# First attention of a two-layer trunk: the two key tiles' scores merged to 128 columns before the exponentials

## The chip, the core and the metric

The kernel runs on one NeuronCore of one Trainium2 chip. The metric is the device time of one execution in microseconds. Before the change the median of three runs is 3507.34 us (3507.19 to 3508.57).

## The reference, cut to what matters

The program computes a two-layer decoder trunk. The first layer is sliding-window attention with learned sinks, on 2048 tokens and 16 meta tokens, 16 query heads of 64 and 2 key heads; after it come routed experts, a second attention, experts again and a final norm. Only the first attention is touched. For a block of 128 queries and one head it computes

```
keys  = [16 meta | 128 of the previous block | 128 of the own block]      # 272 scores
mask  : meta always; previous block where k > q (not for the first block); own block where k <= q
m     = max(max over scores, sink)
p     = exp(s - m) / (sum(exp(s - m)) + exp(sink - m))
o     = p @ values of the 272 keys
```

For one query row, key column c of the previous block is allowed exactly where c > q, and column c of the own block exactly where c <= q. So of each pair of columns (c of the previous, c of the own block) at most one is allowed.

## The kernel before, in words

`attention_a` walks over NT = 17 tiles of 128 rows (tile 0 holds the meta tokens). A tile has 8 pairs (k = 0..7) of two heads, one head of each key head (g = 0, 1), so there are NP = 136 pairs q = 8n + k. Four pairs are one group H of 8 heads. Each engine runs its own written-out list over q; they meet in semaphores only.

In step q the engines do this, in this order:

- TensorE: the scores of pair q into PSUM `S[q % 2]` (L635, three passes for the split of fp32 into high and low part; it waits for `masked` of q - 2). Then one job for a later tile: k = 0, 1 transposes of the input x of tile n + 2 (L576); k = 2, 4, 7 its projection by 512, 512 and 256 columns (L590 to L592, 24 matmuls each); k = 3, 5 transposes of the queries of tile n + 1 (L602), k = 6 of its keys (L608). Then the transposes of the probabilities of pair q - 6 (L649, four of 128x128; after the last pair of a group one more for the meta keys, L654), and the products with the values of pair q - 7 (L668; at a group's end those with the meta values, L677).
- VectorE: scale, mask and row minimum of the negated scores of pair q, one custom instruction for each of the two heads with its read of the accumulator (L538), which gives `z` and `negmax`. At a group's end the argument of the sink's exponential (L544); one step later denominators and reciprocals (L499, L501). Then the job: low parts of x (L452), of the queries (L470) and keys (L479, L480), the bias add after a projection (L461, L464). Then the copy of the transposed probabilities of pair q - 6 out of PSUM, for even pairs (L555), the meta one (L560), and before the scores at q % 4 = 3 the copy of the finished outputs O (L508).
- ScalarE: the job (high parts, L369, L384, L394, L395), the exponentials of pair q with row sums (L431), the sink's (L436), the copy of the transposed probabilities of odd pairs (L444), squares of x (L377, at k = 5).
- GpSimd: scaling of a group's probabilities by the reciprocals (L334 twice, L335), rotary embedding (L321, L322, L324, L351, L358), and the norm's factor (L310, L312).
- SyncE: loads and stores.

There is one PSUM tile PRJ for all the jobs. The second job of a kind waits for VectorE's last read of the first: projection k = 2 for both low parts of x, projection k = 4 for the low part of the queries made at k = 3, projection k = 7 for the low part of the keys made at k = 6, and the transposes of k = 3, 5 and 0 for the bias add before. `PT` is one PSUM tile of two banks, `pT` has three buffers.

Of the kernel before, what the change touches and what calls it, by code (L numbers as in the profile page):

```python
# [16 lines left out]
P = 128  # L17
# [132 lines left out]
def attention_a(nc, io, dram):  # L150


    with ExitStack() as ctx:
# [4 lines left out]
        GW = [512, 512, QKV - 1024]  # L158
        w_hi, w_lo = s.sb("w_hi", [P, DC, QKV], F32R), s.sb("w_lo", [P, DC, QKV], F32R)
# [21 lines left out]
        z = s.sb("z", [P, 2, 2, BAND])  # L181
        prob = s.sb("prob", [P, 3, 4, 2, BAND])
        pmeta = s.sb("pmeta", [P, 2, P])
        pT = s.sb("pT", [P, 3, 4 * P])
        pmT = s.sb("pmT", [P, 2, P])
        negmax = s.sb("negmax", [P, 2, 8])
# [6 lines left out]
        spare = prob[:, :, :, :, :].rearrange("p a i g k -> p (a i g k)")  # L193
        staged = [spare[:, QKV * k:QKV * k + QKV] for k in range(5)]
# [33 lines left out]
        copied_dve, copied_act = s.sem("copied_dve"), s.sem("copied_act")  # L228
# [3 lines left out]
        NCONST = 3  # L232
# [10 lines left out]
        with nc.Block() as block:  # L243
            @block.sync
            def _(sp):
# [30 lines left out]
                sp.dma_start(mask[:, :, :], io["mask_a"].rearrange("(t p) k -> p t k", p=P)).then_inc(consts, 16)  # L276
                load_tables(0)
# [18 lines left out]
            def _(pool):  # L296
# [30 lines left out]
                def scale(H):  # L327
                    pool.wait_ge(den_ready, H + 1)
                    if H >= 2:
                        pool.wait_ge(flipped, 5 * (H - 2) + 5)  # L330
                    heads, by = prob[:, H % 3, :, :, :].rearrange("p i g k -> p (i g) k"), rden[:, H % 2, :, :].rearrange("p i g -> p (i g)")
                    for c in range(2):
                        band = heads[:, 4 * c:4 * c + 4, META:BAND]
                        nc.gpsimd.tensor_tensor(band, band, by[:, 4 * c:4 * c + 4].unsqueeze(2).to_broadcast([P, 4, 2 * P]), ALU.mult).then_inc(scaled, 1)  # L334
# [29 lines left out]
            def _(act):  # L364
# [53 lines left out]
                for q in range(NP + 6):  # L418
                    n, k = divmod(q, PAIRS)
                    job(n, k)  # L420
# [17 lines left out]
                    if 0 <= u < NP:  # L438
                        H, i = divmod(u, 4)
                        if i % 2:  # L440
                            act.wait_ge(flipped, flips(u))
                            if u >= 3:
                                act.wait_ge(summed, pv_count(u - 3))
                            nc.scalar.copy(pT[:, u % 3, :], PT[:, 1, :]).then_inc(copied_act, 1)  # L444
# [4 lines left out]
            def _(dve):  # L449
# [53 lines left out]
                def keep_o(H):  # L503
                    n, b = divmod(H, 2)
                    dve.wait_ge(summed, 5 * H + 5)
                    if n >= 2:
                        dve.wait_ge(o_out[n % 2], 16 * (n // 2))
                    nc.vector.tensor_copy(oT[:, n % 2, 512 * b:512 * b + 512], O[:, :]).then_inc(o_ready, 1)  # L508

# [17 lines left out]
                for q in range(NP + 8):  # L527
                    n, k = divmod(q, PAIRS)
                    if q % 4 == 3 and q >= 11:
                        keep_o((q - 11) // 4)  # L530
                    if q < NP:
                        H, i = divmod(q, 4)
                        dve.wait_ge(scored, q + 1)
                        if q >= 2:
                            dve.wait_ge(exped, q - 1)
                        for g in range(2):
                            j = 2 * i + g
                            last = nc.vector.tensor_tensor_reduce(out=z[:, q % 2, g, :], in0=S[:, q % 2, g, 0:BAND], in1=mask[:, min(n, 2), :],  # L538
                                                                  scale=-A_SCALE, scalar=negsinks[:, 2 * k + g:2 * k + g + 1], op0=ALU.add, op1=ALU.min,
                                                                  accum_out=negmax[:, H % 2, j:j + 1])  # L540
                        last.then_inc(masked, 1)
                        if i == 3:
                            dve.drain()
                            nc.vector.tensor_tensor(sarg[:, H % 2, :], psinks[:, 8 * (H % 2):8 * (H % 2) + 8], negmax[:, H % 2, :], ALU.add).then_inc(sink_in, 1)  # L544
                    if q % 4 == 0 and 4 <= q <= NP:
                        denominators(q // 4 - 1)
                    job(n, k)
                    u = q - 6
                    if 0 <= u < NP:
                        H, i = divmod(u, 4)  # L550
                        if i % 2 == 0:
                            dve.wait_ge(flipped, flips(u))
                            if u >= 3:
                                dve.wait_ge(summed, pv_count(u - 3))
                            nc.vector.tensor_copy(pT[:, u % 3, :], PT[:, 0, :]).then_inc(copied_dve, 1)  # L555
                        if i == 3:
                            dve.wait_ge(flipped, 5 * H + 5)
                            if H >= 2:
                                dve.wait_ge(summed, 5 * (H - 2) + 5)
                            nc.vector.tensor_copy(pmT[:, H % 2, :], PT[:, 0, 0:P]).then_inc(copied_dve, 1)  # L560

            @block.tensor
            def _(pe):
# [60 lines left out]
                for q in range(NP + 7):  # L624
# [15 lines left out]
                    if 0 <= u < NP:  # L640
                        H, i = divmod(u, 4)
                        pe.wait_ge(scaled, 3 * H + 1 + i // 2)
                        if i % 2 == 0 and u >= 2:
                            pe.wait_ge(copied_dve, 3 * H + i // 2)
                        if i % 2 == 1 and u >= 2:
                            pe.wait_ge(copied_act, 2 * H + i // 2)
                        for a in range(4):
                            g, b = divmod(a, 2)
                            last = nc.tensor.transpose(PT[:, i % 2, P * a:P * a + P], prob[:, H % 3, i, g, META + P * b:META + P * b + P], ident[:, :])  # L649
                        last.then_inc(flipped, 1)  # L650
                        if i == 3:
                            pe.wait_ge(scaled, 3 * H + 3)
                            pe.wait_ge(copied_dve, 3 * H + 2)
                            nc.tensor.transpose(PT[:, 0, 0:P], pmeta[:, H % 2, :], ident[:, :]).then_inc(flipped, 1)  # L654
                    u = q - 7
                    if 0 <= u < NP:
                        H, i = divmod(u, 4)
                        m = u // PAIRS
                        if i % 2:
                            pe.wait_ge(copied_act, 2 * H + i // 2 + 1)  # L660
                        else:
                            pe.wait_ge(copied_dve, 3 * H + i // 2 + 1)
# [9 lines left out]
                        if i == 3:  # L672
                            if H == 0:
                                pe.wait_ge(vm_ready, 16 * 8)
                            pe.wait_ge(copied_dve, 3 * H + 3)
# [1859 lines left out]
def shape_constants():  # L2535
# [5 lines left out]
    def table(dim):  # L2541
# [25 lines left out]
        "mask_a": mask.reshape(3 * P, BAND),  # L2567
        "mask_b": np.where(k <= q, 0, MASKED).astype(bf),
# [26 lines left out]
```

## Time and profile before

| What | Value |
|---|---|
| median of three runs | 3507.34 us |
| profiled execution | 3507.11 us, its span 3505.3 us |
| mean granted TensorE clock | 0.946 |
| first attention | first scores at 74.8 us, last output copy ends at 604.9 us |
| busy, whole span | TensorE 90%, VectorE 50%, ScalarE 36%, GpSimd 51% |

The page of the profile gives busy shares over the whole span and in 40 slices of 87.6 us. The first attention is slices 1 to 7. For it the timeline of single engines (start, duration, instruction, and in brackets the idle time before it and what ended that) and the busy times of chosen stretches are read. An instruction's start minus the start of the one before it is what it takes of its engine; its own duration is longer, since instructions overlap.

### The profile page before, as it was taken

The numbers are of one execution on the slowest core, as the hardware profiler recorded it, in microseconds if no ns is written. First come the engines' busy times: TensorE is split into PE (matmuls) and PEld (weight loads), VectorE is DVE, ScalarE is ACT, GpSimd is POOL, SyncE is SP. The second block draws the span as 40 slices with busy tenths as digits, with TensorE's granted clock in tenths as the row PEclk, the third lists the DMA queues.
The fourth block names the chain that finished last, engine by engine and source line by source line (L and its number), as shares of the span: only waits on it lengthen the run. The fifth ranks groups of instructions, "written<-read, shape, count | busy, mean of one in ns | idle before, by whom it ended". The sixth has DMA issues, their size and how long they took to land. (4 is left out here: it accounts for less than half of the span.)

```text
span 3505.3 us, 57395 instructions
## 1 busy us (share of the span) xinstructions
PE 3156.1 (90%) x19855; PEld 2492.3 (71%) x19855; DVE 1742.2 (50%) x3672; ACT 1244.6 (36%) x2673; POOL 1791.3 (51%) x1445
## 2 busy tenths in 40 slices
PE   6999998898799995999799999999998978999950
PEld 4788886787688885898566666666656867888840
DVE  3555555677343333665445555555535653433316
ACT  2444444332222222444344444444343222222212
POOL 2555554344344441454598888888871223444312
PEclk8999999999899997999799999999999989999975
DMA  2001111643898884787410221022005429999818
GB/s 102 27 27 40 39 34 38 210 155 114 302 333 309 301 298 135 236 269 216 113 37 25 52 52 50 13 52 52 10 10 198 161 94 347 363 318 314 276 67 329
DMA packets 358879, 535.93 MB, mean 153 GB/s; under 512 B 82881, under 2 KB 278997, under 8 KB 351780
## 3 DMA queue, kind: packets, MB, share of 16 engines
q1 hardware_dynamic: 331716, 457.26, 40.5%
q0 software_dynamic: 26976, 76.27, 5.6%
q8 instruction: 105, 1.72, 0.2%
q14 instruction: 82, 0.67, 0.1%
HBM read 397.13 MB, written 144.92 MB: 155 GB/s over the span
## 5 line engine op out<-in xcount | busy, mean ns | idle before, releaser
L2105 POOL TENSOR_TENSOR ab_acc<-ab_acc,ab_pT 128x1024 f32<-128x1024 f32 (+2 forms) x320 | 593.6, 1855 | 93.2 <-ACT ab_pT L2139 55.9
L2139 ACT ACTIVATE ab_pT<-ab_S 128x512 f32<-128x512 f32 (+4 forms) x704 | 350.2, 504 | 518.0 <-PE ab_S L2223 252.8
L2155 DVE TENSOR_REDUCE ab_mx<-ab_W 128x2 f32<-128x1024 f32 (+5 forms) x352 | 348.7, 995 | 363.1 <-PE ab_W L2238 219.9
L1264 POOL DMA_INDIRECT scratch_y<-ex_y,ex_prow x64 | 64.8, 1013 | 492.0 <-issue 353.1
L1434 PE MATMUL ex_G<-ex_xT,ex_wg 128*128 128x160 f32 x2048 | 293.3, 302 | 2.6 <-DMA ex_wu<-in_moe_w_up 2.6
L1434 PE MATMUL ex_U<-ex_xT,ex_wu 128*128 128x160 f32 x2048 | 288.6, 299 | 0.0
L1434 PEld LDWEIGHTS ex_G<-ex_xT,ex_wg 128*128 128x128 f32 x2048 | 281.7, 191 | 7.6 <-issue 3.5
L2221 PE MATMUL ab_S<-ab_q_hi,ab_k_hi 97*128 97x512 f32 (+4 forms) x704 | 279.0, 396 | 5.3 <-ACT ab_pT L2139 3.6
L1434 PEld LDWEIGHTS ex_U<-ex_xT,ex_wu 128*128 128x128 f32 x2048 | 281.7, 190 | 0.0
L2275 PE MATMUL ab_O<-ab_pT,ab_v 128*64 128x512 f32 (+3 forms) x1280 | 261.3, 547 | 0.0
L2222 PE MATMUL ab_S<-ab_q_lo,ab_k_hi 96*128 96x512 f32 (+4 forms) x704 | 254.2, 361 | 0.0
L2223 PE MATMUL ab_S<-ab_q_hi,ab_k_lo 96*128 96x512 f32 (+4 forms) x704 | 252.6, 359 | 0.0
L1080 PE MATMUL pr_PR<-pr_wo_hi,pr_o_hi 128*128 128x512 f32 x528 | 217.1, 411 | 34.8 <-DVE pr_wo_lo L947 30.4
L334 POOL TENSOR_TENSOR aa_prob<-aa_prob,aa_rden 128x1024 f32<-128x1024 f32 x68 | 127.3, 1894 | 191.7 <-DVE aa_rden L501 191.7
L2238 PE MATMUL ab_W<-ab_k_hi,ab_q_hi 96*128 96x512 f32 (+5 forms) x704 | 207.1, 378 | 16.4 <-ACT ab_k_hi L2127 14.2
L1305 DVE TENSOR_TENSOR ex_wd_lo<-ex_wd,ex_wd_hi 128x2048 fp32r<-128x2048 f32 x64 | 146.7, 2292 | 137.6 <-ACT ex_wd_hi L1286 100.4
L1082 PE MATMUL pr_PR<-pr_wo_hi,pr_o_lo 128*128 128x512 f32 x528 | 210.0, 398 | 0.0
L1081 PE MATMUL pr_PR<-pr_wo_lo,pr_o_hi 128*128 128x512 f32 x528 | 208.3, 395 | 0.0
L1247 POOL DMA_INDIRECT ex_x<-scratch_xn,ex_grow x64 | 172.0, 2688 | 70.5 <-DVEq L1317 52.8
L2221 PEld LDWEIGHTS ab_S<-ab_q_hi,ab_k_hi 97*128 97x128 f32 x704 | 135.5, 193 | 84.4 <-issue 56.6
L2275 PEld LDWEIGHTS ab_O<-ab_pT,ab_v 128*64 128x64 f32 x1280 | 86.5, 139 | 139.6 <-issue 110.9
L1291 ACT ACTIVATE ex_act_g<-ex_G 128x320 f32<-128x320 f32 x64 | 28.0, 437 | 429.6 <-PE ex_U L1434 429.6
(315 smaller groups left out, 7082.3 us busy)
## 6 DMA issues: line engine op xcount, KB each, us to landing
ex_wg<-in_moe_w_gate SPq DMA_DIRECT2D x64, 1024.0 KB
ex_wu<-in_moe_w_up SPq DMA_DIRECT2D x64, 1024.0 KB
ex_wd<-in_moe_w_down SPq DMA_DIRECT2D x64, 1024.0 KB
pb_y<-scratch_y SPq DMA_DIRECT2D x17, 1024.0 KB
pr_o<-scratch_oT SPq DMA_DIRECT2D x33, 512.0 KB
scratch_h<-pr_h SPq DMA_DIRECT2D x33, 512.0 KB
scratch_xn<-pr_xn SPq DMA_DIRECT2D x33, 512.0 KB, 2.7
fi_y<-scratch_y SPq DMA_DIRECT2D x16, 1024.0 KB, 14.0
```

The source lines that it names most:

```text
L1080: nc.tensor.matmul(PR[:, b, :], o_hi[:, i.slot, c, :], wo_hi[:, c, w], start=(c == 0), stop=False)
L1081: nc.tensor.matmul(PR[:, b, :], o_hi[:, i.slot, c, :], wo_lo[:, c, w], start=False, stop=False)
L1082: return nc.tensor.matmul(PR[:, b, :], o_lo[:, i.slot, c, :], wo_hi[:, c, w], start=False, stop=(c == DC - 1))
L1434: last = nc.tensor.matmul(out[:, f.slot, CAP * k:CAP * k + CAP], w[:, f.slot4, c, P * k:P * k + P], xT[:, f.slot, c, :], start=(c == 0), s ...
L2105: nc.gpsimd.tensor_tensor(to, to, pT[:, U % RING, :, 0:n], ALU.add).then_inc(added, 1)
L2139: nc.scalar.activation(pT[:, U % RING, h, 0:n], S[:, h, 0:n], ACT.Exp, scale=B_SCALE).then_inc(exped, 1)
L2155: nc.vector.reduce_max(mx[:, :, t, c:c + 1].rearrange("p h a -> p (h a)"), W[:, j % 2, :, 0:n], AX.X).then_inc(emptied, 1)
L2221: nc.tensor.matmul(to, k_hi[:, p % 2, h, kb], q_hi[:, p % 2, h, qs], start=True, stop=False)
L2222: nc.tensor.matmul(to, k_hi[0:QD, p % 2, h, kb], q_lo[:, p % 2, h, qs], start=False, stop=False)
L2223: last = nc.tensor.matmul(to, k_lo[:, p % 2, h, kb], q_hi[0:QD, p % 2, h, qs], start=False, stop=not diagonal)
L2238: last = nc.tensor.matmul(W[:, j % 2, h, 0:n], q_hi[0:QD, p % 2, h, P * t:P * t + P], k_hi[0:QD, p % 2, h, lo:lo + n], start=True, stop=no ...
L2275: last = nc.tensor.matmul(O[HD * h:HD * h + HD, G % 2, 512 - n:512], values(U, h), pT[:, U % RING, h, 0:n], start=(U == opens[p, g]), stop ...
```

## The change

The 16 meta columns and the previous block (SPAN = 144 columns) are masked into `z`, the own block's 128 columns into a second tile `zc`, each by its own custom instruction with row minimum; the second takes the first's minimum as its starting value. An elementwise minimum then merges `zc` into `z`. Exponentials, scaling and transposes work on 144 and 128 columns in place of 272 and 256. The transposed probabilities are parted again when they are copied out of PSUM: two multiplications with the 0/1 masks `apart` (bf16), one for each block. That copy is VectorE's for every pair now; the copies of O and of the meta probabilities go to ScalarE.

```diff
+        SPAN = META + P
+        z = s.sb("z", [P, 2, 2, SPAN])
+        zc = s.sb("zc", [P, 2, 2, P])
+        apart = s.sb("apart", [P, 2, P], BF16)
+        stage = s.sb("stage", [P, 5 * QKV])
+        prob = stage[:, 0:3 * 8 * SPAN].rearrange("p (a i g k) -> p a i g k", a=3, i=4, g=2)
 # SyncE
+                sp.dma_start(apart[:, :, :].rearrange("p b q -> p (b q)"), io["apart_a"]).then_inc(consts, 16)
 # GpSimd, scale
-                        band = heads[:, 4 * c:4 * c + 4, META:BAND]
+                        band = heads[:, 4 * c:4 * c + 4, META:SPAN]
 # ScalarE
+                def keep_o(H):
+                    n, b = divmod(H, 2)
+                    act.wait_ge(summed, 5 * H + 5)
+                    if n >= 2:
+                        act.wait_ge(o_out[n % 2], 16 * (n // 2))
+                    nc.scalar.copy(oT[:, n % 2, 512 * b:512 * b + 512], O[:, :]).then_inc(o_ready, 1)
+                    if q % 4 == 3 and q >= 11:
+                        keep_o((q - 11) // 4)
...
-                            nc.scalar.copy(pT[:, u % 3, :], PT[:, 1, :]).then_inc(copied_act, 1)
+                    if 0 <= u < NP and u % 4 == 3:
+                        act.wait_ge(flipped, 5 * H + 5)
+                        nc.scalar.copy(pmT[:, H % 2, :], PT[:, 0, 0:P]).then_inc(copied_m, 1)
 # VectorE, pair q
-                            last = nc.vector.tensor_tensor_reduce(out=z[:, q % 2, g, :], in0=S[:, q % 2, g, 0:BAND], in1=mask[:, min(n, 2), :],
-                                                                  scale=-A_SCALE, scalar=negsinks[:, 2 * k + g:2 * k + g + 1], op0=ALU.add, op1=ALU.min,
-                                                                  accum_out=negmax[:, H % 2, j:j + 1])
-                        last.then_inc(masked, 1)
+                            nc.vector.tensor_tensor_reduce(out=z[:, q % 2, g, :], in0=S[:, q % 2, g, 0:SPAN], in1=mask[:, min(n, 2), 0:SPAN],
+                                                           scale=-A_SCALE, scalar=negsinks[:, 2 * k + g:2 * k + g + 1], op0=ALU.add, op1=ALU.min,
+                                                           accum_out=before[:, H % 2, j:j + 1])
+                        dve.drain()
+                        for g in range(2):
+                            nc.vector.tensor_tensor_reduce(out=zc[:, q % 2, g, :], in0=S[:, q % 2, g, SPAN:BAND], in1=mask[:, min(n, 2), SPAN:BAND],
+                                                           scale=-A_SCALE, scalar=before[:, H % 2, j:j + 1], op0=ALU.add, op1=ALU.min,
+                                                           accum_out=negmax[:, H % 2, j:j + 1])
+                        dve.drain()
+                        nc.vector.tensor_tensor(z[:, q % 2, :, META:SPAN], z[:, q % 2, :, META:SPAN], zc[:, q % 2, :, :], ALU.min).then_inc(masked, 1)
 # VectorE, pair u = q - 6
-                            nc.vector.tensor_copy(pT[:, u % 3, :], PT[:, 0, :]).then_inc(copied_dve, 1)
+                        for b in range(2):
+                            last = nc.vector.tensor_tensor(pT[:, u % 3, :].rearrange("p (g b q) -> p b g q", g=2, b=2)[:, b, :, :],
+                                                           PT[:, u % 2, 0:2 * P].rearrange("p (g q) -> p g q", g=2),
+                                                           apart[:, b, :].unsqueeze(1).to_broadcast([P, 2, P]), ALU.mult)
+                        last.then_inc(copied, 1)
 # TensorE, pair u = q - 6
-                        for a in range(4):
-                            g, b = divmod(a, 2)
-                            last = nc.tensor.transpose(PT[:, i % 2, P * a:P * a + P], prob[:, H % 3, i, g, META + P * b:META + P * b + P], ident[:, :])
+                        for g in range(2):
+                            last = nc.tensor.transpose(PT[:, i % 2, P * g:P * g + P], prob[:, H % 3, i, g, META:SPAN], ident[:, :])
```

The semaphores `copied_dve` and `copied_act` become `copied` (one count for each pair) and `copied_m` (one for each group). TensorE's products with the values are as before: four of 128x64 weights for each pair, and four with the meta values for each group.

## Rows read from the trace of the kernel before

**Rows 1.** Busy time by engine in one tile's stretch; then TensorE's clock:

```profile
303.98:336.17 32.19, 32.19 (x253) 26.02 (x251) 17.38 (x56) 14.57 (x48) 17.74 (x17) 1.00 0.11 36
```

**Rows 2.** Timeline of TensorE, the same tile: start, duration, line, operation:

```profile
303.98 0.50 PE L590 MATMUL aa_PRJ<-aa_w_hi,aa_x_hi 128*128 128x512 f32 x1
...
309.56 0.60 PE L649 MATMUL aa_PT<-aa_ident,aa_prob 128*128 128x128 f32 x4
...
311.77 0.40 PE L635 MATMUL aa_S<-aa_k_hi,aa_q_hi 64*128 64x272 f32 x2
...
314.52 0.50 PE L590 MATMUL aa_PRJ<-aa_w_hi,aa_x_hi 128*128 128x512 f32 x1
...
320.11 0.60 PE L649 MATMUL aa_PT<-aa_ident,aa_prob 128*128 128x128 f32 x4
...
321.23 0.39 PE L635 MATMUL aa_S<-aa_k_hi,aa_q_hi 64*128 64x272 f32 x2
...
327.03 0.39 PE L590 MATMUL aa_PRJ<-aa_w_hi,aa_x_hi 128*128 128x256 f32 x1
...
334.37 0.60 PE L649 MATMUL aa_PT<-aa_ident,aa_prob 128*128 128x128 f32 x4
334.81 0.27 PE L654 MATMUL aa_PT<-aa_ident,aa_pmeta 128*128 128x128 f32 x1
...
336.17 0.50 PE L590 MATMUL aa_PRJ<-aa_w_hi,aa_x_hi 128*128 128x512 f32 x1
```

**Rows 3.** Timeline of VectorE, the same tile:

```profile
309.76 0.75 DVE L461 SCALAR_TENSOR_TENSOR aa_qk<-aa_PRJ,aa_rstd,aa_bqkv 128x512 f32<-128x512 f32 x1 [4.74 <-PE aa_PRJ L592]
...
326.63 0.68 DVE L555 COPY aa_pT<-aa_PT 128x512 f32<-128x512 f32 x1
327.23 0.68 DVE L508 COPY aa_oT<-aa_O 128x512 f32<-128x512 f32 x1
...
328.25 0.50 DVE L538 CUSTOM_DVE_ANT_0 aa_z<-aa_S,aa_mask,aa_negsinks 128x272 f32<-128x272 f32 x1
328.67 0.08 DVE L538 DVE_READ_ACCUMULATOR2_ANT aa_negmax<- 128x1 f32 x1
328.84 0.17 DVE L544 TENSOR_TENSOR aa_sarg<-aa_psinks,aa_negmax 128x8 f32<-128x8 f32 x1
```

**Rows 4.** Groups by shape on VectorE, whole span: busy, mean ns, idle before:

```profile
L1305 DVE TENSOR_TENSOR ex_wd_lo<-ex_wd,ex_wd_hi 128x2048 fp32r<-128x2048 f32 x64 | 146.7, 2292 | 137.6 <-ACT ex_wd_hi L1286 100.4 <-issue 37.2
L1305 DVE TENSOR_TENSOR ex_h_lo<-ex_h,ex_h_hi 128x256 fp32r<-128x256 f32 x64 | 27.2, 425 | 5.0
L1022 DVE CUSTOM_DVE_ANT_0 pr_junk<-pr_hot,pr_place 128x32 f32<-128x32 f32 x66 | 12.7, 192 | 7.6
```

**Rows 5.** Timeline of a later stage, GpSimd and VectorE side by side:

```profile
779.57 2.39 POOL L870 TENSOR_TENSOR pr_res<-pr_res,pr_bo 128x1024 f32<-128x1024 f32 x1
...
779.62 3.43 DVE L1037 SCALAR_TENSOR_TENSOR pr_xn<-pr_h,pr_rstd,pr_gain 128x1024 f32<-128x1024 f32 x1 [1.29 <-POOL pr_rstd L880]
```

**Rows 6.** Timeline of GpSimd in the tile of rows 2:

```profile
321.14 1.27 POOL L321 TENSOR_TENSOR aa_rot<-aa_qk,aa_cs 128x512 f32<-128x512 f32 x1 [1.02 <-DVE aa_qk L461]
...
323.79 2.37 POOL L324 TENSOR_TENSOR aa_qk<-aa_qk,aa_cs 128x1024 f32<-128x1024 f32 x1
326.30 2.39 POOL L351 TENSOR_TENSOR aa_qr<-aa_qk,aa_rot 128x1024 f32<-128x1024 f32 x1
```

**Rows 7.** Timeline of TensorE at the stage's start:

```profile
79.70 0.50 PE L590 MATMUL aa_PRJ<-aa_w_hi,aa_x_hi 128*128 128x512 f32 x1 [0.82 <-DVE aa_x_lo L452]
...
88.40 0.52 PE L590 MATMUL aa_PRJ<-aa_w_hi,aa_x_hi 128*128 128x512 f32 x1 [0.83 <-DVE aa_q_lo L470]
...
92.13 0.41 PE L590 MATMUL aa_PRJ<-aa_w_hi,aa_x_hi 128*128 128x512 f32 x1
```

**Rows 8.** Busy time and clock in half a microsecond there, columns as rows 1:

```profile
89.00:89.50 0.50, 0.50 (x2) 0.39 (x2) 0.41 (x4) 0.28 (x1) 0.00 (x0) 0.50 0.00 0
```

**Rows 9.** L538 in the last two tiles: durations ns min/median/max, first and last start:

```profile
L538 DVE CUSTOM_DVE_ANT_0 aa_z<-aa_S,aa_mask,aa_negsinks x32: 491/498/501, 557.4 to 591.8; 128x272 f32<-128x272 f32 x32
```

More of the change, by code:

```diff
@@ L185, in attention_a @@
         pmT = s.sb("pmT", [P, 2, P])
+        before = s.sb("before", [P, 2, 8])
         negmax = s.sb("negmax", [P, 2, 8])
@@ L192, in attention_a @@
         oT = s.sb("oT", [P, 2, DC * P])
-        spare = prob[:, :, :, :, :].rearrange("p a i g k -> p (a i g k)")
-        staged = [spare[:, QKV * k:QKV * k + QKV] for k in range(5)]
+        staged = [stage[:, QKV * k:QKV * k + QKV] for k in range(5)]
         NS = len(staged)
@@ L231, in attention_a @@
         o_out = s.sems("o_out", 2)
-        NCONST = 3
+        NCONST = 4
         def live(n):
@@ L416, in _ @@
                         square(2)
-                for q in range(NP + 6):
+                def keep_o(H):
[4 more added lines that the diff above has]
+                    nc.scalar.copy(oT[:, n % 2, 512 * b:512 * b + 512], O[:, :]).then_inc(o_ready, 1)
+                for q in range(NP + 8):
                     n, k = divmod(q, PAIRS)
+                    if q % 4 == 3 and q >= 11:
+                        keep_o((q - 11) // 4)
                     job(n, k)
@@ L525, in _ @@
                     job(-1, k)
-                for q in range(NP + 8):
+                for q in range(NP + 6):
                     n, k = divmod(q, PAIRS)
-                    if q % 4 == 3 and q >= 11:
-                        keep_o((q - 11) // 4)
                     if q < NP:
@@ L549, in _ @@
                     if 0 <= u < NP:
[L550 to L554, printed above, removed]
-                            nc.vector.tensor_copy(pT[:, u % 3, :], PT[:, 0, :]).then_inc(copied_dve, 1)
[L556 to L560, printed above, removed]
+                        dve.wait_ge(flipped, flips(u))
+                        if u >= 3:
+                            dve.wait_ge(summed, pv_count(u - 3))
+                        for b in range(2):
[3 more added lines that the diff above has]
+                        last.then_inc(copied, 1)
             @block.tensor
@@ L642, in _ @@
                         pe.wait_ge(scaled, 3 * H + 1 + i // 2)
[L643 to L646, printed above, removed]
-                        for a in range(4):
-                            g, b = divmod(a, 2)
-                            last = nc.tensor.transpose(PT[:, i % 2, P * a:P * a + P], prob[:, H % 3, i, g, META + P * b:META + P * b + P], ident[:, :])
+                        if u >= 2:
+                            pe.wait_ge(copied, u - 1)
+                        if i == 0 and H >= 1:
+                            pe.wait_ge(copied_m, H)
+                        for g in range(2):
+                            last = nc.tensor.transpose(PT[:, i % 2, P * g:P * g + P], prob[:, H % 3, i, g, META:SPAN], ident[:, :])
                         last.then_inc(flipped, 1)
```

32 lines of the change are left out of this document (10 added, 22 removed).

## The prediction

> **What bounds the kernel now.** I went from the page's 40 slices, where the first attention is slices 1 to 7 and has TensorE at 9, to the busy times of one tile: from one projection k = 2 to the next it takes 32.19 us, TensorE is busy in all 32.19 of them at the full clock, VectorE in 17.38, ScalarE in 14.57, GpSimd in 17.74 [rows 1]. The first reading is therefore that TensorE bounds the stage and that a saving on it counts in full. The timeline says how long that stays true. A tile is three projections with short work between them: the first from 303.98 to 309.56 (5.58 us), a gap A of other work to 314.52 (4.96 us), the second to 320.11 (5.59), a gap B to 327.03 (6.92), the third, some 2.97 us, and a gap C of 6.17 to 336.17 [rows 2]. VectorE's idle time lies behind the projections: 4.74 us before the bias add at 309.76 [rows 3]. Its idle time can't be used in the gaps, because all projections share one PSUM tile and each waits for VectorE's last low part before it. So the question for each gap is which is longer, TensorE's work in it or VectorE's chain through it.
>
> **TensorE's part.** Two of four transposes go from each pair. Four take 0.44 us (334.37 to 334.81 [rows 2]), so one is 0.11 and the stage saves 16 x 0.11 = 1.7 us a tile, 272 x 0.11 = 29 us in all. Scores and products are the same.
>
> **VectorE's part.** Now a mask of 272 columns takes 0.42 us of the engine (328.25 to 328.67 [rows 3]), 0.84 a pair. A column costs 1.04 ns ((2292 - 425) / 1792 [rows 4]). A mask of 144 columns is then 0.42 - 0.13 = 0.29, one of 128 is 0.27. For the fixed part the 32-column instruction bears me out: 192 ns from SBUF against 497 ns, and 240 columns are 250 of the 305 ns between them [rows 4, 9]. A drain after the accumulator's read lets the next start 0.17 us after it (328.67 to 328.84 [rows 3]); I take 0.18. The minimum over 256 columns with both inputs in SBUF lasts 425 ns [rows 4]; overlapping the next instruction by the same 0.085 as the copy does (0.68 long, next 0.60 later [rows 3]) it takes 0.34. The block is 2 x 0.29 + 0.18 + 2 x 0.27 + 0.18 + 0.34 = 1.82 us in place of 0.84. Its bounds: 1.5 if a drain behind these costs almost nothing, 2.0 if the shorter masks don't shrink as the slope says. The copy out of PSUM becomes two multiplications of 256 columns, 0.34 each by the same row: 0.68 for every pair in place of 0.60 for every second. That a broadcast bf16 mask costs more than fp32 no row shows; bounds 0.60 to 0.90 a pair. The moves to ScalarE take off 0.60 and about 0.20 each four pairs.
>
> **The gaps with both.** I walk each gap with these durations, counting from the projection's end, 0.05 us for a handoff, and the jobs as they last now.
>
> A: scores 3 start 2.21 later [rows 2], now 2.00; done and seen at 2.7. Mask block, 4.5. Drain and sink argument, 0.34. Low part of the queries, 0.69. The second projection starts at 5.6, now 4.96. The bias add and the copy (1.35) are hidden before 2.7.
>
> B: scores 5 start at 1.12 - 0.21 = 0.9 [rows 2], seen at 1.6. Mask 5 to 3.4, low part of the queries to 4.0, copy to 4.7, mask 6 to 6.5, low part of the keys, 7.05. TensorE is later: its transposes of step 6 now wait for the meta copy, which is ScalarE's and queued behind exponential 5 (masked at 3.5, exponentials 0.84, copy 0.27, so 4.7). Then transposes 0.32, values 0.59, meta values 1.09, scores 7 0.57: the third projection starts at 7.3, now 6.92.
>
> C: scores 0 seen at 1.6, mask 0 to 3.4, denominators 0.38, low part of x 0.60, copy 0.68, mask 1 1.81, low part 0.69: 7.6, now 6.17.
>
> A tile becomes 5.58 + 5.6 + 5.59 + 7.3 + 2.97 + 7.6 = 34.65 us, 2.45 more. TensorE's 1.7 us is gone in its waits. Fourteen full tiles give +34. The first tile has no copies yet: +1. In the last two there are no projections; their 16 masks start from 557.4 to 591.8 [rows 9], 2.27 us apart. VectorE then needs 1.82 + 0.68 a pair, (0.34 + 0.38) / 4 for the sinks and 1.6 / 16 for the last queries and keys: 2.77, so 15 x 0.5 = 7.5, and 1.5 for the way of the last pairs. Sum of the chain: +45. Its bounds by the block (four of a tile's eight are on the path and all of the last 16, so 0.1 us on it moves 4 x 15 x 0.1 + 1.6 = 7.6 us): 1.5 gives +21; 2.0 gives +59, with the dear copy (0.2 on two to four of a tile) some +68.
>
> **What the minimum meets on GpSimd.** Its form is new in this stage: two inputs in SBUF. At 779.62 a VectorE instruction with two SBUF inputs starts 0.05 after a GpSimd one that lasts 2.39, and takes 3.43 us [rows 5]; its 1024 columns are 0.425 + 768 x 1.04 ns = 1.22 us [rows 4], so it stood 2.2 still, the other's whole time but for an overlap. I take every meeting as a full wait for the other's end. The masks of now, with one input in PSUM, are never longer than 0.50 [rows 9]. GpSimd's rotary work follows the second bias add: from 321.14, 1.03 after the projection's end, two instructions of 1.27, then 2.37 and 2.39 [rows 2, 6]. Counted from that end they fill 1.0 to 3.6, 3.7 to 6.05 and 6.2 to 8.6. The minimum of mask 5 comes at 3.07, in the second: 0.5 us of wait. The one of mask 6 comes 3.1 us after that wait's end, 6.65: GpSimd's last, moved 0.3 by VectorE's turn, started at 6.5. If the minimum is behind it, it waits 2.2, if a little before, 0. Bounds per tile 0 and 2.7; I take 0.5 + 1.1 = 1.6 for 15 tiles, +24. Scaling (halved to 0.95 an instruction) and the rest meet the other blocks for some tenths only.
>
> The Trainium skill (SBUF — State Buffer, "SBUF: two separate sides") says the pair of ports that VectorE and GpSimd share is held for a whole instruction and the other engine blocks fully. The trace agrees, with its 3.43 us. By the rule the 24 us stand; were the ports shared by bandwidth, it would be some tenths a tile and the sum 20 us lower.
>
> **What the waits do to the clock.** TensorE waits 1.1 us before the second projection, about 1 or more before the third, twice 1.1 before the first. At the stage's start waits of this kind are seen: after 0.82 us the projection at 79.70 runs fast; the one at 88.40, after 0.83 and another 0.37 some 2 us before, goes to half [rows 7], granted clock 0.50, the level of 1.2 GHz [rows 8]. Its first nine matmuls take 3.73 us (88.40 to 92.13), at 0.23 each they would take 2.07: 1.7 us lost, on the path. Bounds per tile: none to all three, 0 to 5. I take one, 15 x 1.65 = +25.
>
> The skill's page TensorE: Matmul & The Clock Gate ("HAM oscillation") wants long idle gaps for a fall, longer than any here, and says in its next section that short ones between groups of matmuls can do it too. By the first sentence alone the sum would be 25 us lower; the row at 88.40, which fell after 0.83, goes with the second.
>
> **Sum.** The profiled execution took 3507.11 us, 0.2 under the median, so one base serves. 3507 + 45 + 24 + 25 = **3601 us**. Costs at nothing: the fourth constant's load (0.5 us of cover before the first bias add; 1 us without), the copy of O on ScalarE (idle behind each projection), shorter exponentials and scaling (nobody waits for them).
>
> **Rivals.** *Chain alone.* Mask 6's minimum passes before GpSimd's last instruction and the clock holds: 3507 + 45, 3552 us. For it: the second projection at 79.70 ran fast after 0.82, and 0.2 us decides the 2.2. *All of it.* Every tile pays 2.7 us at the port and three slow starts: 45 + 38 + 74, 3664 us. For it: a tile repeats itself, so a bad phase does too. Against: a late clock moves the phases. *TensorE still bounds.* The mask blocks lie beside TensorE's work and the 29 us come in full: 3478 us. It needs a block below some 1.0 us; at 1.2 us the gaps A to C sum to now's 18.05 and the stage is even. Against: two masks of 272 alone take 0.84, and the block has four, two drains and a minimum. *It does nothing,* within 0.2% (7 us, which is what measurement can tell): block near 1.25 and the port free.
>
> **Chances.** Forecast 0.42, chain alone 0.26, all of it 0.21, TensorE bounds 0.04, nothing 0.03, more than all 0.04. The range must reach from the chain alone with a cheap block and some of the other two (3507 + 21 + 17) to all of it: 3545 to 3664. Faster 0.04, same 0.03, slower 0.93.
>
> **What would show it.** L538's successors: starts 0.29 and 0.27 apart, the minimum 1.47 after the first. The minimum's median 0.43 and maximum above 2 us. Tile period 36 to 39 us, TensorE busy some 30.5 of it, waits before all three projections on the low parts. A clock of 1.00 through 200 to 400 us would refute the 25, a maximum of the minimum under 0.5 the 24. A period below 32.2, with VectorE still waiting for TensorE at each mask, would refute the chain, and with it the sign.

## The result and the profile after

The changed kernel takes 3594.05 us (median of 4 runs, 3589.9 to 3599.68), the kernel before 3507.95 beside it; the ratio is 1.0242, interval 1.0224 to 1.0261. It is slower by 86 us, 8 less than the forecast's 94. The profiled execution took 3592.99 us.

One tile, from one first projection to the next, as [rows 1] show it for before. Busy time by engine (TensorE, its weight loads, VectorE, ScalarE, GpSimd), then the granted clock:

```profile
297.50:333.94 36.44, 30.99 (x235) 24.27 (x236) 26.55 (x105) 12.59 (x47) 14.34 (x16) 1.00 0.10 32
```

The tile grew from 32.19 to 36.44 us. TensorE, busy in all of it before, is now idle for 5.4 us; VectorE went from 17.38 to 26.55 busy. TensorE's timeline of that tile (start, duration, line, operation, and in brackets idle time and who ended it), to be laid beside [rows 2]:

```profile
297.46 0.50 PE L598 MATMUL aa_PRJ<-aa_w_hi,aa_x_hi 128*128 128x512 f32 x1 [0.86 <-DVE aa_x_lo L465]
...
303.05 0.38 PE L656 MATMUL aa_PT<-aa_ident,aa_stage 128*128 128x128 f32 x2
...
308.55 0.50 PE L598 MATMUL aa_PRJ<-aa_w_hi,aa_x_hi 128*128 128x512 f32 x1 [0.91 <-DVE aa_q_lo L483]
...
314.13 0.38 PE L656 MATMUL aa_PT<-aa_ident,aa_stage 128*128 128x128 f32 x2
...
318.70 0.30 PE L616 MATMUL aa_PRJ<-aa_ident,aa_qr 128*128 128x128 f32 x1 [0.96 <-DVE aa_q_lo L483]
...
323.41 0.39 PE L598 MATMUL aa_PRJ<-aa_w_hi,aa_x_hi 128*128 128x256 f32 x1 [1.56 <-DVE aa_k_lo L493]
...
326.38 0.38 PE L656 MATMUL aa_PT<-aa_ident,aa_stage 128*128 128x128 f32 x2
...
330.86 0.66 PE L584 MATMUL aa_PRJ<-aa_ident,aa_x 128*128 128x128 f32 x4 [0.97 <-DVE aa_x_lo L465]
...
333.94 0.50 PE L598 MATMUL aa_PRJ<-aa_w_hi,aa_x_hi 128*128 128x512 f32 x1 [0.87 <-DVE aa_x_lo L465]
```

The three gaps between projections are now 5.50 (303.05 to 308.55), 9.28 (314.13 to 323.41) and 7.56 us (326.38 to 333.94). Before they were 4.96, 6.92 and 6.17. Each ends with TensorE waiting for a low part that VectorE makes. VectorE's block of a pair, and the two minima that meet GpSimd, in the same tile:

```profile
305.72 0.37 DVE L542 CUSTOM_DVE_ANT_0 aa_z<-aa_S,aa_mask,aa_negsinks 128x144 f32<-128x144 f32 x1 [1.06 <-PE aa_S L643]
306.02 0.36 DVE L542 CUSTOM_DVE_ANT_0 aa_z<-aa_S,aa_mask,aa_negsinks 128x144 f32<-128x144 f32 x1
306.50 0.35 DVE L548 CUSTOM_DVE_ANT_0 aa_zc<-aa_S,aa_mask,aa_before 128x128 f32<-128x128 f32 x1
...
306.78 0.35 DVE L548 CUSTOM_DVE_ANT_0 aa_zc<-aa_S,aa_mask,aa_before 128x128 f32<-128x128 f32 x1
...
307.21 0.43 DVE L552 TENSOR_TENSOR aa_z<-aa_z,aa_zc 128x256 f32<-128x256 f32 x1
...
317.20 0.76 DVE L552 TENSOR_TENSOR aa_z<-aa_z,aa_zc 128x256 f32<-128x256 f32 x1
...
320.62 2.34 DVE L552 TENSOR_TENSOR aa_z<-aa_z,aa_zc 128x256 f32<-128x256 f32 x1
```

and GpSimd's rotary work beside them, which answers to [rows 6]:

```profile
316.39 1.28 POOL L327 TENSOR_TENSOR aa_rot<-aa_qk,aa_cs 128x512 f32<-128x512 f32 x1
317.81 2.36 POOL L329 TENSOR_TENSOR aa_qk<-aa_qk,aa_cs 128x1024 f32<-128x1024 f32 x1
320.32 2.35 POOL L356 TENSOR_TENSOR aa_qr<-aa_qk,aa_rot 128x1024 f32<-128x1024 f32 x1
```

The free minimum takes 0.43 us. The one at 317.20 falls into GpSimd's instruction of 316.39 and ends 0.29 after it (0.33 longer than the free one); the one at 320.62, started 0.30 behind a GpSimd instruction, also ends 0.29 after it (1.91 longer). The whole stage, by the durations (min/median/max in ns) of the minimum and by the copies of O, the last of which ends the stage:

```profile
L552 DVE TENSOR_TENSOR aa_z<-aa_z,aa_zc x136: 424/426/2353, 74.9 to 673.6; 128x256 f32<-128x256 f32 x136
...
L428 ACT COPY aa_oT<-aa_O x34: 559/585/587, 122.4 to 687.4; 128x512 f32<-128x512 f32 x34
```

So the stage ends at 688.0 us, 83.1 later than the 604.9 of before; the rest of the span is 2.8 us longer. Of the 83.1, 65.9 are there at the last projection (L598's last start, 621.1 us; before 555.2), and 17.2 come behind it.

### The profile page after: what moved, and what is told of

It reads as the page before. It is cut to its first block and busy times, and to the rows that moved or that the text cites. A ratio compares the mean times of both kernels' runs of the same rounds, so it can differ in the third digit from the quotient of the medians.

```text
span 3591.2 us, 57940 instructions
## 1 busy us (share of the span) xinstructions
PE 3149.6 (88%) x19583; PEld 2475.2 (69%) x19583; DVE 1892.9 (53%) x4488; ACT 1211.5 (34%) x2673; POOL 1734.6 (48%) x1445
## 5 line engine op out<-in xcount | busy, mean ns | idle before, releaser
L598 PE MATMUL aa_PRJ<-aa_w_hi,aa_x_hi 128*128 128x512 f32 (+1 forms) x408 | 157.7, 387 | 65.4 <-DVE aa_k_lo L493 24.0
L339 POOL TENSOR_TENSOR aa_stage<-aa_stage,aa_rden 128x512 f32<-128x512 f32 x68 | 69.3, 1040 | 288.6 <-DVE aa_rden L514 288.6
```

## The experiments

In the text "stage end" is the end of the last copy of O, and "tile" the time from one 128x512 projection to the same one of the next tile, which repeats within 0.1 us while the clock holds, but for up to three tiles of an execution that are 0.2 to 0.4 us longer.

**The port.** The second pair of masked scores goes to free columns of the score bank, so the minimum has one input in SBUF instead of two.

```
-   tensor_tensor_reduce(out=zc[:, q % 2, g, :], in0=S[..., SPAN:BAND], ...)
+   tensor_tensor_reduce(out=S[:, q % 2, g, BAND:BAND + P], in0=S[..., SPAN:BAND], ...)
-   tensor_tensor(z[..., META:SPAN], z[..., META:SPAN], zc[:, q % 2, :, :], ALU.min)
+   tensor_tensor(z[..., META:SPAN], z[..., META:SPAN], S[:, q % 2, :, BAND:BAND + P], ALU.min)
```

> The changed kernel with one thing different: the second pair of masked scores (the tile's own block) is written into the free columns of the score bank in PSUM instead of into SBUF, so the minimum has only one SBUF input; all instructions and waits stay. Port theory (the minimum of the block after mask 5, and of the one after mask 6, stands still behind GpSimd's two-input instruction, 0.33 + 1.92 us in the tile looked at): both minima shrink to about 0.43 us, gap B falls from 9.28 to about 7.3 us, 2.0 us a tile times 14 or 15, so about 3565 us (3560 to 3571). Rival, the long minima lie beside other work and gap B is longer for another reason: 3592 to 3596. Rival, a PSUM output makes the second masking pair slower by 0.05 us a block and eats 4 us of it: about 3569.

Measured: 3567.84 us, ratio 1.0162 (1.0145 to 1.0179), stage end 666.6. That lies in the port theory's 3560 to 3571; the rival with the dearer PSUM output (3569) fits as well, and both turn out to be true. The minimum by its durations, and one tile by its second projections:

```profile
L552 DVE TENSOR_TENSOR aa_z<-aa_z,aa_S x136: 420/422/424, 78.2 to 653.5; 128x256 f32<-128x256 f32 x136
```

```profile
303.65 0.50 PE L598 MATMUL aa_PRJ<-aa_w_hi,aa_x_hi 128*128 128x512 f32 x1 [0.95 <-DVE aa_q_lo L483]
...
338.37 0.50 PE L598 MATMUL aa_PRJ<-aa_w_hi,aa_x_hi 128*128 128x512 f32 x1 [0.95 <-DVE aa_q_lo L483]
```

No minimum lasts over 0.424 us any more, and the tile is 34.72 us instead of 36.46, 1.74 less. The port's price is a little higher than that: gap B fell from 9.28 to 7.39, by 1.89, while the second masking pair's PSUM output made the block 0.04 longer and gaps A and C 0.05 and 0.09 (5.55 and 7.65). What is left, 34.72 against the forecast's 34.65, is the chain.

**What a block costs.** One more instruction in each block ahead of the minimum.

```
+   tensor_tensor(zc[:, q % 2, :, :], S[:, q % 2, :, 0:P], mask[:, 0:2, 0:P], ALU.min)
    tensor_tensor(z[..., META:SPAN], ..., ALU.min)
```

> The kernel of e1_psum plus one more VectorE instruction in every block ahead of the minimum (256 columns, one PSUM and one SBUF input, its output unused), worth 0.3 to 0.4 us of VectorE by the minimum's own 0.43 us. It measures what a block costs. Chain theory (TensorE's waits ahead of the three projections each hold one or more blocks, 7.6 us for each 0.1 us): 23 to 30 us above e1_psum. Rival, the added length lies beside TensorE's work: 0 to 5 us above. Rival, the longer waits make TensorE's clock fall as the forecast's third term has it: 25 us more on top, 48 to 55 above e1_psum, with granted clocks below 0.97 between 100 and 500 us.

Measured: 3601.18 us, ratio 1.0260 (1.0243 to 1.0277), 33 us above the kernel of the port test (23 to 30 expected); stage end 694.9.

```profile
312.92 0.50 PE L599 MATMUL aa_PRJ<-aa_w_hi,aa_x_hi 128*128 128x512 f32 x1 [1.28 <-DVE aa_q_lo L483]
...
349.10 0.50 PE L599 MATMUL aa_PRJ<-aa_w_hi,aa_x_hi 128*128 128x512 f32 x1 [1.28 <-DVE aa_q_lo L483]
```

The minimum starts 1.88 after the block's first instruction instead of 1.54, so the block is 0.33 longer. The tile goes to 36.15 at the full clock, the wait before the second projection from 0.95 to 1.28: the added time is a wait of TensorE, one for one. The stage is 28.3 us longer, and 3.0 of these are two tiles in which the clock fell (37.6 and 37.8 us; the other 11 of 13 take 36.1 to 36.5). The 25.3 that are left are 7.7 for each 0.1 us of block, where the forecast had 7.6. The rival of the clock did not come as 25 us: between 120 and 620 us the granted clock leaves the full level only from 361 to 365 and from 398 to 402 us. It did not fall behind the longest waits of a tile, which are 1.28 and 1.35 us here, but behind those of 1.01 and 1.21 us for the low part of the queries, in the product that follows; the second of the two:

```profile
397.09 0.30 PE L617 MATMUL aa_PRJ<-aa_ident,aa_qr 128*128 128x128 f32 x1 [1.21 <-DVE aa_q_lo L483]
...
398.50 2.07 PE L682 MATMUL aa_O<-aa_pmT,aa_vmeta 128*128 128x128 f32 x8
```

**Where TensorE takes over.** Three kernels in which the own block's scores are left out of the softmax, so that the block is short: alone, and with one and two such instructions ahead of the masks.

```
    for g in range(2):
-       tensor_tensor_reduce(... 0:SPAN ..., accum_out=before[...])
+       tensor_tensor_reduce(... 0:SPAN ..., accum_out=negmax[...])
-   (second pair and the minimum)
+   (one or two 256-column instructions ahead, in the second and third kernel)
```

> Leaves out the own block's scores from the softmax altogether: of the changed kernel's mask block only the first two instructions stay (meta and previous tile, 144 columns), the second pair and the minimum are gone, so the block is near 0.58 us where the kernel before has 0.84; transposes, parting and all copies are those of the changed kernel. If halving the transposes is worth what the forecast says (272 transposes of 0.107 us, 29 us), and the block is all that stood in its way, TensorE bounds again: about 3478 us (3472 to 3486). Rival, the moved copies or the parting cost something by themselves: 3490 to 3507. Rival, the transposes lay beside a wait anyway: 3500 to 3507.

> The kernel of e3_short (own block's scores left out of the softmax) plus one 256-column VectorE instruction a pair ahead of the two masking instructions (output unused), so the block is about 0.93 to 1.0 us. Read by the end of the attention stage alone (578.5 us in e3_short, 604.9 in the kernel before, 688.0 in the changed one), since its wrong scores route the experts' tokens differently later. The forecast said that TensorE still bounds below 1.0 us, even at 1.2: then the stage ends within 4 us of 578.5. Rival, the chain slope of e2_longer (28 us of stage for one such instruction) holds from the start: about 606 us.

> The same with two such instructions, block about 1.3 to 1.4 us, read by the end of the stage. With the measured slope (28 us for one instruction) drawn back from e1_psum (block 1.8 us, stage end 666.6 us) a block of 1.35 us ends at 666.6 minus 28 times 0.45/0.35 = 631 us, and the knee lies where this line meets 578.5, at a block of about 0.7 us. By the forecast's own sum (7.6 us for each 0.1 us, TensorE's bound until 1.2) it would be about 590 us.

The whole times (3591.18, 3598.26 and 3623.76 us) can't be read: what follows the stage took 3011 to 3015 us in all three instead of 2900. The likely reason, not shown by itself, is that the routing of the tokens to experts follows from the scores that were left out. The first expectation overlooked this, and its 3478 us can't be tested. The stage can be read. One tile of each, by 128x512 projections:

```profile
303.39 0.50 PE L591 MATMUL aa_PRJ<-aa_w_hi,aa_x_hi 128*128 128x512 f32 x1
...
334.24 0.50 PE L591 MATMUL aa_PRJ<-aa_w_hi,aa_x_hi 128*128 128x512 f32 x1
```

```profile
302.60 0.50 PE L592 MATMUL aa_PRJ<-aa_w_hi,aa_x_hi 128*128 128x512 f32 x1
...
333.58 0.50 PE L592 MATMUL aa_PRJ<-aa_w_hi,aa_x_hi 128*128 128x512 f32 x1
```

```profile
316.36 0.50 PE L593 MATMUL aa_PRJ<-aa_w_hi,aa_x_hi 128*128 128x512 f32 x1 [0.32 <-DVE aa_q_lo L483]
...
348.55 0.51 PE L593 MATMUL aa_PRJ<-aa_w_hi,aa_x_hi 128*128 128x512 f32 x1 [0.33 <-DVE aa_q_lo L483]
```

| kernel | block, start of the first to end of the last | tile | stage end |
|---|---|---|---|
| own block left out | 0.66 | 30.85 | 578.5 |
| and one more | 0.98 | 30.97 | 581.9 |
| and two more | 1.32 | 32.20 | 610.9 |
| port test | 1.96 | 34.72 | 666.6 |
| port test, longer block | 2.28 | 36.15 | 694.9 |

The table is nearly two straight pieces. Up to about 1.0 us the tile is flat, and TensorE is busy in 30.94 and 30.84 of the 31 us from 303 to 334; beyond it the tile rises by 3.9 us for each us of block between 1.32 and 1.96, and by 4.5 from there, about the four blocks that the forecast had on the path. The second of the three met its expectation (within 4 us of 578.5), the third lay between its two (590 and 631). At a block of 1.32 the tile is 32.20, the same as before's 32.19: there the saved transposes are exactly used up. The flat piece is also the saving: the stage ends 26.4 us earlier than before, where the forecast had 29. A tile gives 1.34 us of this where the forecast had 1.7, so two transposes fewer save 0.17 us a pair and not 0.21; the rest comes at the start and behind the last projection, where other work is shorter too. It also settles that the parting and the moved copies cost the tile nothing by themselves while the block is short.

**The merge behind the exponentials.** Mask and exponentials stay at 272 columns; GpSimd adds the two blocks' probabilities, one of which is zero, and scales the 128 columns.

```
    band = heads[:, 4 * c:4 * c + 4, META:SPAN]
+   nc.gpsimd.tensor_tensor(band, band, heads[:, 4 * c:4 * c + 4, SPAN:BAND], ALU.add)
+   pool.drain()
    nc.gpsimd.tensor_tensor(band, band, by[...], ALU.mult)
```

> Merges behind the exponentials instead of ahead of them: mask and exponentials over 272 columns as in the kernel before (one pair of instructions on VectorE, no minimum); GpSimd adds the two blocks' probabilities (one of the two is zero in every place) and then scales 128 columns a head; two transposes a pair, parting and copies as in the changed kernel. GpSimd's work for four heads goes from 1.89 us to about 1.28 + 0.1 + 1.04 = 2.4. TensorE's saving stays and the chain is that of the kernel before: about 3480 us (3475 to 3490). Rival, GpSimd becomes late: its scaling ends at 320.1 in the tile looked at and the rope starts at 321.14, so 1.1 us a head group eats the slack and the key's and queries' flips come up to 1 us a tile later: 3490 to 3505. Rival, the parting on VectorE delays the next block: 3507 or more.

Measured: 3492.83 us, ratio 0.9958 (0.9943 to 0.9974), stage end 588.9. The 3475 to 3490 of the theory were missed, and the time lies in the range of the first rival. Measured a second time:

> The kernel of e4_merge_late again, beside the kernel before in five rounds, since 18 us separate it from before and f4_early_add, a near twin, came out at 0.9981 where this had 0.9958. Theory: 0.995 to 0.997, 3490 to 3498 us, the stage's end within 2 us of 588.9. Rival: the twin's number is the true one, 0.998 to 1.000.

3492.32 us, ratio 0.9953 (0.9940 to 0.9967): as expected, and the rival is out. The stage end, 591.6, missed its 2 us by 0.7; the last projection came 5.0 us later and the part behind it was 2.3 us shorter. This version beats both kernels, by 15 to 19 us against before.

```profile
302.85 0.50 PE L591 MATMUL aa_PRJ<-aa_w_hi,aa_x_hi 128*128 128x512 f32 x1
...
334.00 0.50 PE L591 MATMUL aa_PRJ<-aa_w_hi,aa_x_hi 128*128 128x512 f32 x1
```

Its tile is 31.15 us, no wait before these projections; the block is that of before, 0.93. It is 0.3 a tile and 8.6 us behind the last projection (6.3 in the second trace) worse than the kernel with the short block. Of the 8.6, 3.4 lie in the last 16 blocks, whose starts span 33.9 us instead of 30.5. The kernel with the block of 0.98 has 33.7 there without any adds, so this part goes with the longer block. Another 5.1 (2.8 in the second trace) come behind the last block. There GpSimd's two adds with their drains, 2.8 us in sum, lie between the last block and the transposes, and in the first trace the clock was at 0.59 from 575 to 585 us, 0.87 in the second. The idea of the adds alone was tried by putting them ahead of GpSimd's wait for the denominators:

> The kernel of e4_merge_late with GpSimd's adds put ahead of its wait for the denominators: they need the exponentials alone. In e4_merge_late the stage ends at 588.9 us, 10.4 later than in e3_short, 8.6 of it after the last projection, where a head group's scaling waits for the adds. If that is the cause, 1.3 to 2.7 us come off the last groups: stage end 583 to 587, about 3489 us. Rival, the adds now collide with VectorE's sum and reciprocal or the GpSimd order delays the rope: no gain, 3492 to 3497. It would be the fastest version so far.

3500.65 us (11 runs, 3493 to 3508), ratio 0.9981 (0.9970 to 0.9992), stage end 591.7, tile 31.17. There is no gain, and the median is above the rival's 3492 to 3497 too. That does not clear the adds, since the edit put both of them ahead of the first scaling. Behind the last projection TensorE now waits once for that scaling, the clock falls to half behind this wait, and VectorE gets its scores 6.16 us after the block before, instead of 3.33:

```profile
542.93 0.69 PE L656 MATMUL aa_PT<-aa_ident,aa_prob 128*128 128x128 f32 x2 [1.43 <-POOL aa_prob L346]
...
547.70 0.50 DVE L549 CUSTOM_DVE_ANT_0 aa_z<-aa_S,aa_mask,aa_negsinks 128x272 f32<-128x272 f32 x1 [3.29 <-PE aa_S L643]
```

**The clock behind the last projection.** TensorE gets work in its waits there.

```
    last.then_inc(scored, 1)
    job(n, k)
+   if n >= NT - 1:
+       for c in range(2):
+           nc.tensor.matmul(PRJ[:, :], x_hi[:, c, :], w_hi[:, c, 0:512], start=True, stop=True)
```

> The changed kernel plus, in the last 15 turns of the loop (the last tile's eight pairs and what follows), two 128x512 matmuls a turn on TensorE behind the scores, into the projection bank that nobody reads any more: 0.46 us at the full clock, less than TensorE waits there. It asks whether the slow clock after the last projection is what made the tail 17.2 us longer instead of 9. In the changed kernel the granted clock is 0.78 to 0.83 between 620 and 680 us, and VectorE waits 2.55 us for scores behind eight matmuls that took 2.08 us instead of 1.16. Clock theory: the clock is 0.95 or more there, the end of the stage comes 5 to 9 us earlier, about 3587 us. Rival, the tail is VectorE's block alone and the slow matmuls lie beside it: within 2 us of 3594. Rival, the filler itself delays the transposes: slower, 3597 or more.

> The changed kernel as it is, beside the others on one chip, to read two things: whether f1_fill's 1.0257 and the changed kernel's 1.0242 differ (theory: they don't, 1.023 to 1.026), and how many falls of the clock below 0.98 its steady tiles show in another execution (3 such stretches of 10 us before 610 us in the first trace besides the first tile's, 5 in f1_fill's), with the tile periods that go with them: if a fall costs what the forecast took, 1.65 us, the tile with it is that much longer; if it lies beside VectorE's work, less than 0.3 us.

> The kernel of e4_merge_late plus the filler of f1_fill (two 128x512 matmuls a turn behind the scores in the last 15 turns). In e4_merge_late the granted clock is 0.59 from 575 to 585 us and 0.80 from 585 to 590; in f1_fill the filler held it at 0.96 to 1.00 where the changed kernel had 0.66 to 0.83, and the part behind the last projection took 63.2 us instead of 66.9. If the clock costs there what it cost in f1_fill, the stage ends 3 to 5 us earlier than in g3_late_again. Rival: in these last turns TensorE's own work is on the path, so the filler costs what it gives: within 1 us, or up to 5 us later.

The changed kernel's meta values product in this part and the scores that VectorE gets behind it, first as it is, then with the filler:

```profile
656.60 2.08 PE L681 MATMUL aa_O<-aa_pmT,aa_vmeta 128*128 128x128 f32 x8
...
659.62 0.37 DVE L542 CUSTOM_DVE_ANT_0 aa_z<-aa_S,aa_mask,aa_negsinks 128x144 f32<-128x144 f32 x1 [2.55 <-PE aa_S L643]
```

```profile
662.24 1.16 PE L684 MATMUL aa_O<-aa_pmT,aa_vmeta 128*128 128x128 f32 x8
```

Its clock by stretches, with the filler; the filler starts at 654.3 us:

```profile
620.00:640.00 20.00, 15.77 (x119) 12.71 (x115) 14.35 (x60) 5.83 (x24) 6.91 (x9) 0.79 0.07 27
640.00:660.00 20.00, 15.99 (x140) 11.07 (x139) 17.90 (x86) 7.73 (x32) 4.97 (x6) 0.96 0.07 27
660.00:680.00 20.00, 16.94 (x138) 11.52 (x137) 16.49 (x78) 7.82 (x34) 4.00 (x6) 1.00 0.07 28
```

In the last tile the blocks start 2.78, 2.84, 2.49 and 3.35 us apart with the filler, 2.77, 2.84, 2.48 and 5.32 in the changed kernel: where the clock has fallen, the fourth turn takes 2.0 us more. The first of the three long turns (5.39 us) came before the filler started. The part behind the last projection took 63.2 us instead of 66.9 (65.0 in the changed kernel's second trace), 1.8 to 3.7 less where 5 to 9 were expected. The whole time did not follow, neither to the theory's 3587 nor clearly to one of the rivals: 3596.4 us, ratio 1.0257 (1.0243 to 1.0271), against 3594.2 and 1.0252 (1.0238 to 1.0266) for the changed kernel in its second set of runs; these two do not differ, as was expected of them. The filler's execution reached the last projection 6.3 us later than the first trace of the changed kernel, and 0.9 later than its second; the code up to there is the same. Of the 6.3, falls of the clock in full tiles are 3.0 (three against one, next section), the rest lies before and in the first tile. In the kernel with the late merge the filler is a loss: 3501.36 us, ratio 0.9977 (0.9967 to 0.9987). The stage ends at 588.5 us, 3.1 earlier than in the twin beside it, as the theory had it, but not by the filler: the last projection, ahead of it, came 4.0 us earlier, and the part behind took 51.4 us where the twin took 50.6. So the rival holds there. The span behind the stage is 2911 us where the twin has 2899. Why is open.

## Why the prediction was right, and where not

The forecast was 3601 us, measured were 3594. Sign, chain and port were right; the clock's term was not, and the total came as near as it did because that error was met by others of the opposite sign. By the forecast's own terms, in us, from the profiled executions:

| step | forecast | measured | from |
|---|---|---|---|
| chain, 14 full tiles | 34 | 35.4 | 14 x (34.72 - 32.19) |
| port | 24 | 24.4 | 14 x (36.46 - 34.72) |
| clock up to the last projection | 25 | 2.8 | one tile of 37.98 (1.5), the last projection (1.3) |
| start, first tile and what is left | 1 | 3.3 | 65.9 less the three above |
| behind the last projection | 9 | 17.2 | 66.9 against 49.7 |
| rest of the span | 0 | 2.8 | 2903.2 against 2900.4 |

The forecast's column sums to 93; its chain was entered as 45, where its parts give 44.3. The last row is no finding: the same code behind the stage took 2899 to 2905 us in the other executions and 2911 in one. Nor are the first two rows exact, because the port test's block was 0.04 longer: with 0.14 us a tile moved from one to the other, the chain is 33 and the port 26.

**The block** came as worked out: successors 0.30 and 0.28 apart, the minimum 1.49 after the first where 1.47 was foretold, 0.43 long. (The forecast counts the block by what it takes of VectorE, 1.82; the tables here count to the end of the last instruction, 1.92, since instructions overlap.) The slope of the column price and the drain's 0.17 [rows 3, 4] carried over to shapes that the trace of before did not have. The broadcast bf16 mask cost nothing extra: the multiplications have a mean of 413 to 415 ns.

**The gaps** A (5.6 against 5.50) and C (7.6 against 7.56) are right to 0.1 us, and the sum of the chain is 34.65 against 34.72. In B, TensorE's own way was 7.3 us in the forecast and is 7.39 with the port free, with no wait before the third projection. With the port the forecast had 7.3 and 1.6, 8.9; measured 9.28.

**TensorE's saving** did exist and did vanish in waits. "It needs a block below some 1.0 us" is near the table's knee, which by the forecast's way of counting lies at about 0.9. "Even at 1.2" is right in the same way: the tile is even at 1.32 to the end of the last instruction, some 1.25 as the forecast counts.

**The port.** Rows 5 and 6 gave the right place and nearly the right price: the minimum of mask 5 stood 0.33 (0.5 foretold), that of mask 6 1.91, which the forecast had as 2.2 or nothing, with half of it taken. It was no matter of chance. The forecast had GpSimd's last instruction moved by 0.3 to 6.5 us after the projection; it stayed at 6.19, and the minimum came at 6.49. All 14 full tiles have the long wait (one of 1.45 is in the first). The minimum's 136 instructions stood 33 us in all (mean 667 ns). Of the 2.24 us a tile only 1.89 reached its length, because VectorE's own chain in gap B was 7.05 us by the forecast and TensorE's 7.3: the difference covers a part. The forecast added its wait to the longer of the two. So the term's near hit (24 against 24 to 26) has two errors in it that partly cancel, half a wait too few and the cover left out.

By the Trainium skill (SBUF — State Buffer, "SBUF: two separate sides") the pair of ports is held for a whole instruction. The runs agree: 1.91 us of standstill where both of the minimum's inputs are in SBUF, and none of the 136 over 0.424 us when one is in PSUM.

**The clock: this step failed.** "I take one" slow start a tile, 1.65 us each, 25 us in all; measured were 2.8. The price was about right and the count was not. Behind the longest wait, 1.56 us, the clock falls in some tiles only. The changed kernel, its third projection at 396.35 and the clock by the us (columns as above):

```profile
396.35 0.45 PE L598 MATMUL aa_PRJ<-aa_w_hi,aa_x_hi 128*128 128x256 f32 x1 [1.57 <-DVE aa_k_lo L493]
```

```profile
395.00:396.00 1.00, 0.00 (x0) 0.00 (x0) 1.00 (x2) 0.07 (x1) 0.86 (x2) 1.00 0.00 0
396.00:397.00 1.00, 0.65 (x3) 0.66 (x4) 1.00 (x5) 1.00 (x5) 0.55 (x1) 0.76 0.00 0
397.00:398.00 1.00, 1.00 (x7) 1.00 (x6) 0.89 (x7) 0.30 (x1) 0.00 (x0) 0.50 0.00 0
```

That tile took 37.98 instead of 36.46 us, 1.5 more. In the 14 tiles behind the first the wait before the third projection is 1.55 to 1.57 us each time. The clock fell behind this one and behind the last, at 617.28, which lies past the 13 whole tile periods between 125 and 603 us, and held behind the other twelve. The forecast had named a clock of 1.00 from 200 to 400 us as what would refute its 25; it was 0.99. Of the 13 periods one has a fall in this trace, four in the second trace of the changed kernel and three in the filler's, and the last projection fell in all three. With the longer block two fell. In the port test none did; its waits there are at most 1.03 us, but for one of 1.37 and one of 1.22. So two to five falls of about 1.5 us, 3 to 7 us, not 25. The error came from taking the stage's start [rows 7, 8] as a sample of the steady tiles: there too one of two like waits had been harmless. The rule of the Trainium skill that the forecast weighed against this (TensorE: Matmul & The Clock Gate, "HAM oscillation", long gaps for a fall) was nearer for the full tiles, though waits of 1.57 and 1.56 us did do it in this trace.

**Behind the last projection** the pace at the full clock, read from the filler's trace, is 2.87 us a pair over four turns of the last tile (2.78, 2.84, 2.49, 3.35), foretold 2.77. Over the last 16 blocks it was 3.25, 48.8 us for 15 steps against 34.0 before. Three turns of the fourth kind took 5.39, 5.32 and 4.43 us instead of 3.35, 5.1 us together: the forecast had no clock term there, and in this trace it was worth more than in all the tiles. The work after the last block took 15.8 us instead of 13.5, 2.3 more where 1.5 was foretold. The forecast was 22 us too high for the clock in the tiles, 8 too low behind the last projection, 2 at the start and 5 in the other rows, so that, with the 1 us of its rounding, 8 were left. That this is so small is luck; the sign never hung on it.

Open: why the clock falls behind some waits of 1.56 us and not behind others, and with the longer block behind 1.01 us and not behind 1.35; whether the late merge's adds can be had for less; why the code behind this stage, the same in all, took 2911 us with the late merge's filler and 2899 to 2905 otherwise.

## What to carry to other kernels

- When a busy engine's work is cut at the price of more work on another, look for the chain that starts as soon as the busy one has to wait: with four blocks a tile on it, 1 us of block costs 4 us, and a flat stretch ends sharply (here at 1.0 us of block).
- Price a new instruction by where its inputs lie. The same minimum took 0.43 us or 2.34, by whether GpSimd was in a two-input instruction; one operand in PSUM took this away.
- A merge can be put where an engine has slack: behind the exponentials on GpSimd the same halving of transposes gained 0.45% instead of losing 2.4%.

## What the runs showed that was not expected

A fall of the clock that costs 1.5 us in a full tile costs 2.0 in a turn of the last tile, because there scores and the meta values product are themselves on VectorE's path. Where falls come is not fixed by the program: the same code had one, four and three of them in 13 tiles, and with the last projection two, five and four behind 14 equal waits. A masking instruction that writes to PSUM is followed by an accumulator read of 142 ns instead of 82, and the block grew by 0.04 us only.
